# Four 64x64-tile matmuls a pick, and no VectorE adds, for the value rows of a two-layer decoder trunk

## The reference, cut to what matters

```python
def peer_ffn(h, w_q, sub_keys, u_tab, v_tab):
    ...   # scores against two sets of 128 keys, top 16 of each, top 16 of their sums:
    experts = i1 * PEER_KEYS + i2
    gates = jax.nn.softmax(best_s, axis=-1)
    ...   # chunks of 128 tokens, hk = 8 heads * 16 picks = 128
    def chunk(args):
        hh, ee, gg = args
        u_sel = u_tab[ee].astype(jnp.float32)
        v_sel = v_tab[ee].astype(jnp.float32)
        act = jax.nn.gelu(jnp.einsum('td,tkd->tk', hh, u_sel))
        return jnp.einsum('tk,tkd->td', gg * act, v_sel)

for l in range(DEPTH):
    x = mixer_sublayer(x, ...)
    x = x + peer_ffn(rms_norm(x, norm2_g[l]), peer_wq[l], peer_keys[l], peer_u[l], peer_v[l])
```

## Time and profile before

| | |
|---|---|
| median of 3 runs | 1670.06 us (1668.13 to 1670.81) |
| the profiled execution's own time | 1670.59 us |
| its span, first to last instruction | 1668.8 us |
| TensorE busy, share of the span | 78% |
| VectorE | 72% |
| ScalarE | 26% |
| GpSimd | 41% |
| HBM read | 621.15 MB, 373 GB/s over the span |
| mean granted TensorE clock | 0.901 of 2.4 GHz |

### The profile page before, as it was taken

The page is one execution under the profiler, slowest core; times in us unless marked ns, Lnnn a source line. Parts: engine busy times, 40 slices in busy tenths (PEclk is TensorE's granted clock), DMA queues, the critical chain, the costliest instruction groups (busy, mean ns, idle before and its releaser), DMA issues. The chain is left out here.

```text
span 1668.8 us, 15094 instructions
## 1 busy us (share of the span) xinstructions
PE 1308.3 (78%) x4636; PEld 732.2 (44%) x4636; DVE 1209.0 (72%) x2831; ACT 432.8 (26%) x1021; POOL 677.2 (41%) x791
## 2 busy tenths in 40 slices
PE   7794776977696697878878777889878788776786
PEld 6664432433354344544355434545345433332332
DVE  3834999865599978767589987867679975555555
ACT  3211331341233321224133332135123321111111
POOL 6002223686175253344333243434432235444441
PEclk9898998988798898988989888989989979999999
DMA  9006998969998899999999999999999989999998
GB/s 387 18 29 265 418 374 334 392 258 367 421 407 351 328 420 419 420 421 419 420 398 420 411 345 420 420 419 420 420 401 420 402 319 422 420 419 420 420 420 334
DMA packets 86050, 623.21 MB, mean 373 GB/s; under 512 B 9808, under 2 KB 9808, under 8 KB 10960
## 3 DMA queue, kind: packets, MB, share of 16 engines
q0 software_dynamic: 73728, 536.90, 78.9%
q1 hardware_dynamic: 12240, 85.33, 12.5%
HBM read 621.15 MB, written 1.05 MB: 373 GB/s over the span
## 5 line engine op out<-in xcount | busy, mean ns | idle before, releaser
L1348 PE MATMUL acc<-slot,diag 128*128 128x512 f32 x1780 | 870.1, 644 | 226.9 <-ACT diag L734 226.9
L458 POOL DMA_INDIRECT slot<-experts,idx x512 | 577.9, 1129 | 950.3 <-PE acc L1348 785.4
L1041 DVE CUSTOM_DVE_ANT_0 slot<-slot,h 128x1024 f32<-128x1024 f32 x512 | 611.8, 1226 | 273.1 <-DMA slot<-experts,idx 271.5
L1348 PEld LDWEIGHTS acc<-slot,diag 128*128 128x128 f32 x1780 | 358.1, 207 | 689.4 <-issue 419.8
L734 ACT ACTIVATE diag<-cst,ge 128x128 f32<-128x128 f32 x445 | 144.2, 391 | 187.0 <-DVE ge L760 185.8
L725 ACT ACTIVATE ge<-ge 128x4 f32<-128x4 f32 x129 | 26.5, 205 | 466.0 <-DVE ge L1041 465.1
L1318 PE MATMUL PB<-hT,ring 128*128 128x128 f32 x1024 | 126.2, 284 | 4.6 <-ACT hT L698 4.1
L1318 PEld LDWEIGHTS PB<-hT,ring 128*128 128x128 f32 x1024 | 122.8, 200 | 6.5 <-ACT hT L698 5.5
L719 ACT ACT_TABLE_LOAD x31 | 39.8, 1283 | 203.1 <-DVE rs L1000 203.1
L1059 DVE SCALAR_TENSOR_TENSOR xs<-slot,ge,xs 128x1024 f32<-128x1024 f32 x67 | 86.1, 1285 | 2.4
L725 ACT ACT_TABLE_LOAD x56 | 71.8, 1283 | 29.3 <-DVE ge L1041 28.4
(11 more groups left out here) (229 smaller groups left out, 1148.4 us busy)
## 6 DMA issues: line engine op xcount, KB each, us to landing
ring<-weights SPq DMA_DIRECT2D x32, 1152.0 KB, 9.5
ring<-weights SPq DMA_DIRECT2D x28, 1024.0 KB, 9.2
slot<-weights SPq DMA_DIRECT2D x12, 1024.0 KB, 22.2
slot<-experts,idx POOLq DMA_INDIRECT x512, 16.1
sml<-small SPq DMA_DIRECT2D x2, 1160.0 KB, 10.0
xs<-x SPq DMA_DIRECT2D x2, 512.0 KB, 8.1
out<-xs SPq DMA_DIRECT2D x4, 256.0 KB, 5.1
tabp<-tabs SPq DMA_DIRECT2D x2, 268.0 KB, 9.2
```

What stands on the lines that cost most here:

```text
L458: pool.indirect_dma_start(out=slot[:, E % SLOTS, :], out_offset=None, in_=experts, in_offset=bass.IndirectOffsetOnAxis(ap=idx[:, n % 2, e: ...
L1041: ins = dve.tensor_tensor_reduce(u, u, h2[:, n % 2, :], 1.0, 0.0, ALU.mult, ALU.add, d[:, i:i + 1])
L1348: ins = pe.matmul(acc[:, half, :], diag[:, d % DIAGS, :], slot[:, E % SLOTS, D + half * 512:D + half * 512 + 512], start=(E % PICKS == 0), ...
```

## The change

- `added` returns only the last two picks of all: 65 picks go from VectorE to TensorE, each with a diagonal on ScalarE.
- The diagonal is folded: a new constant `fold` has two 64 x 64 identities one above the other, and a pick's matrix is 128 x 64. Its rows 0 to 63 are the diagonal for tokens 0 to 63, its rows 64 to 127 that for tokens 64 to 127.
- A pick is added by four matmuls of 64 x 64 stationary and 512 columns: token half i (rows of the array) and column half (columns of the array). Token half i goes to PSUM bank i, column half to partitions 0 to 63 or 64 to 127 of it. The last of the four tells `expert_done`.
- The drain puts this back: four adds of 64 partitions x 512 in place of two of 128 x 512.

```diff
-    routing, experts = False, {PICKS * STEPS - 2, PICKS * STEPS - 1}
-    for kind, a, b in ORDER:
-        if kind == "open":
-            routing = a == STEPS - 1
-        elif kind == "close" and not routing:
-            experts.add(experts_of(a, b)[-1])
-        elif kind == "mix" and a.startswith("route"):
-            routing = True
-    return experts
+    return {PICKS * STEPS - 2, PICKS * STEPS - 1}
...
-        diag = sb("diag", [P, DIAGS, P])
+        diag = sb("diag", [P, DIAGS, HALF])
...
-                    act.activation(diag[:, d % DIAGS, :], ident, ACT.Copy,
+                    act.activation(diag[:, d % DIAGS, :], c_("fold"), ACT.Copy,
...
                 for half in range(2):
-                    x_half = xs[:, n % 2, half * 512:half * 512 + 512]
-                    told(tt(x_half, x_half, acc[:, half, :], ALU.add), "drained")
+                    for i in range(2):
+                        x_part = xs[HALF * i:HALF * i + HALF, n % 2, half * 512:half * 512 + 512]
+                        ins = tt(x_part, x_part, acc[HALF * half:HALF * half + HALF, i, :], ALU.add)
+                    told(ins, "drained")
...
-                    for half in range(2):
-                        ins = pe.matmul(acc[:, half, :], diag[:, d % DIAGS, :],
-                                        slot[:, E % SLOTS, D + half * 512:D + half * 512 + 512],
-                                        start=(E % PICKS == 0), stop=(d + 1 == by_tensor(PICKS * (n + 1))),
-                                        skip_group_check=True)
+                    for i in range(2):
+                        rows = slice(HALF * i, HALF * i + HALF)
+                        for half in range(2):
+
+                            ins = pe.matmul(acc[HALF * half:HALF * half + HALF, i, :], diag[rows, d % DIAGS, :],
+                                            slot[rows, E % SLOTS, D + half * 512:D + half * 512 + 512],
+                                            start=(E % PICKS == 0), stop=(d + 1 == by_tensor(PICKS * (n + 1))),
+                                            skip_group_check=True)
                     ins.then_inc(S["expert_done"], 1)
...
+    put("fold", np.concatenate([np.eye(HALF)] * 2))
```

More of the change, by code:

```diff
@@ L25 @@
 KD = D // P
+HALF = P // 2
 SEQ = 256
@@ L53 @@
 for _name, _w in (("ident", P), ("mask", P), ("ones", P), ("band", 4 * P), ("prev", 64), ("first", 64),
-                  ("iota", TOPK), ("minus", HEADS), ("eps", 1)):
+                  ("iota", TOPK), ("minus", HEADS), ("eps", 1), ("fold", HALF)):
     CONST[_name] = (_at, _at + _w)
```

## The result

Median of five runs 1658.2 us (1656.39 to 1660.04) against 1668.13 us (1665.75 to 1670.81) of the kernel before, five runs of each: ratio 0.994, 95% interval 0.9928 to 0.9952. It is faster, by 10 us where 18 were forecast; 1658.2 lies in the range, 6 us above the predicted 1652.

What follows compares the result with a forecast made beforehand. DMA engines were taken as full at 420 GB/s in most slices, so gains come only from slices below that. The terms -6.0 - 1.8 - 2.5 - 3.6 + 1.0 - 6.4 + 1.4 sum to -17.9: predicted 1652 us, range 1640 to 1665.

Steps and rivals of the forecast that it cites:

- Quads 7 to 12: Quads 7 to 11 of n = 0: VectorE works without a gap, so removing five adds of 1.20 gives -6.0 us.
- The price of a pick: TensorE's adds: four tiles side by side make a pick cost 0.86 us in place of 1.71.
- rival 3: TensorE's four tiles take turns, a pick costs 3.43 us and TensorE bounds: some 2,200 us; chance 0.07.
- what would show it: Signs if right: TensorE's adds 430 to 450 us busy, 0.86 us a pick, drain waits near 0, among others.
- Rival 1: A pick still costs 1.71 us, from a halved clock or tiles two at a time: 1661 us; chance 0.17.
- The gathers behind: GpSimd's last gather ahead of the tables: quad 12's four picks done after 3.4 us, not three after 5.1: -1.8 us.
- GpSimd's tables: Layer 1's tables: five VectorE adds each hold GpSimd up by 0.8 to 1.0 us; -2.5 us, bounds -4.5 and 0.
- Quad 23 and the projection: Quad 23's add delays routing dots, three times: -3.6 us; query projection in n = 1 and n = 2 may lose clock: +1.0.
- The add of quad 22 gives nothing: Removing quad 22's add gains nothing, since VectorE then waits for TensorE's query projection and ScalarE's copy.
- The step ends: Ends of three steps: first gather 1.7 us sooner each, -1.3 more at n = 1's end from the drain: -6.4 us.
- The end: Last drain: four adds take 2.8 us in place of two at 1.41, with nothing to cover it: +1.4 us.
- Rival 2: VectorE and GpSimd meet elsewhere: a 6.59 us stall comes once more, no gain on the tables: 1661 us; chance 0.13.

Runs made afterwards that it cites:

- (2): The kernel before, with TensorE doing the 65 picks by its old two matmuls and nothing packed: 1666.05 us, ratio 0.9981 to the kernel before.
- (7): The changed kernel with four more matmuls of zeros after each pick, to double its price: 1673.88 us, ratio 1.0028 to the kernel before.
- experiments 3: The changed kernel with VectorE adding the last pick of quads 13 to 18 of n = 0, ahead of the dots: 1666.15 us, ratio 0.998.
- 4: As experiments 3, but each of the six adds stands behind the four dots of the next quad: 1660.81 us, ratio 0.9936 to the kernel before.
- experiments 8: The changed kernel with TensorE adding the picks of quad 22 ahead of the query projection, not behind it: 1656.56 us, ratio 0.9922.
- 9: The changed kernel with the picks ahead of the query projection for n = 2 and n = 3 alone: 1656.97 us, ratio 0.9933.
- second profile: The same changed kernel measured and profiled once more, nothing changed: 1659.34 us, ratio 0.9939 to the kernel before.
- experiment 12: The changed kernel with picks ahead of the projection (n = 2, 3), the last step's picks as before, and zero matmuls without a wait: 1652.91 us.

## Why the prediction was right, and where not

- **Quads 7 to 12, and what bounds there:** right. -6.0 forecast, -6.0 in both profiles, and 6.1 us come back when these five adds do.
- **The price of a pick:** its mechanism was right (0.86 forecast without the tail, 0.86 measured so at the high clock, 0.915 with the tail; rival 3 is out), and what would show it was not: 607 us busy, not 430 to 450. The estimate took the high clock throughout; the low one stood in the working only as a rival. The rule of the Trainium skill that it named (TensorE: Matmul & The Clock Gate, "Why this matters for your kernels") speaks of just this: gaps send TensorE back to half rate. The trace agrees, with a mean clock of 0.83 in place of 0.901. Rival 1 took it as halved everywhere; it was so in part. Its time was too low, too: it gave 1661 us for the old price of a pick, and the two experiments with that price took 1666 (2) and 1674 (7).
- **The gathers behind:** -1.8 forecast, -1.4 and -0.9 measured; with the price doubled the term turns to +4.0, from -6.1 to -2.1, where the rival had +0.5.
- **GpSimd's tables:** mis-sized. -2.5 with a bound of -4.5 was forecast, -8.6 and -6.3 measured. The step that failed is "each holding GpSimd up by 0.8 to 1.0 us": besides its own hold, an add ahead of the dots makes them hold more, 15 to 17 operations in the stretch against 10 to 13 without adds (experiments 3 and 4). How it does so is open.
- **Quad 23 and the projection:** -3.6 and +1.0 forecast. Both parts show. The projection takes 6.63 us in n = 1 and 5.92 in n = 2, 5.57 and 5.18 before, and from w(., 22) to w(., 23) 1.1 and 0.8 us are lost; from w(., 23) to w(., 24) the 1.2 us of the add are gained (-16.0 to -17.2, and -15.6 to -16.9). In n = 0 quad 23 gains 1.4 us. But then quad 25 loses 4.9 and 4.2 us in the first profile, 3.3 and 3.7 in the second. The step that failed is that the gain of quad 23 was taken as kept in n = 1 and n = 2, where the mixing quads were called "as full" throughout: the DMA engines run short behind the projection, before as well, and a wait for rows at quad 25 was put at nothing. "The add of quad 22 gives nothing" held, as its slot stood fourth in line. This loss is the largest thing that the prediction didn't see; it comes with the packing and experiments 8 and 9 take it away, and what lies between the packing and the late rows is open.
- **The step ends:** -6.4 forecast; -1.7, -3.2 and -3.1 measured (-8.0; the second profile -2.1, -2.7, -2.7). The drain waits went to 2.54 us (n = 0) and 1.51 (n = 1), not near 0, for the low clock: where quad 31's picks ran at the high one (experiment 12) they are 0.04.
- **The end:** +1.4 forecast, +1.3 measured.
- **Rival 2** did not come: VectorE's one stall of 6.59 us became two, of 2.83 and 4.78 us, in the same part of n = 0.

The measured terms of the first profile, -6.0 - 1.4 - 8.6 + 9.1 - 8.0 + 1.3 = -13.6, make nearly all of the -14.4 of the span. Two errors partly met: 4 to 6 us too little at the tables, and 7 to 9 us of loss at quad 25 not seen. That the total came within 4 us of the forecast -17.9 is luck to that extent. The median lies 1.8 us above the profiled execution, and the forecast had put it 0.5 below, which makes up the rest of the 6.

## What to carry to other kernels

When work moves from one engine to another, follow each gain to the next place where the transfers run short, since it can be lost there. When two traces are compared, line them up by the work and not by the clock: a window at the same time shows other work once one kernel is 17 us ahead. Cost a long operation on VectorE by what it does to GpSimd through the operations behind it as well, and measure that by putting it back in another place. And where TensorE's share falls, take durations at both clocks for what stands behind its idle times; what counted here was when a pick was done behind an idle time, and not how many could be done in the whole.

## What the runs showed that was not expected

- Tiles that are a part of the array both ways run four at a time in float32: a pick of four 64 x 64 x 512 matmuls took 0.86 us (0.915 with the tail), where one of two 128 x 128 x 512 took 1.71 (1.78).
- Packing TensorE's adds from 1.96 to 1.19 us a pick gave 39% of their busy time, not half: the mean clock fell from 0.901 to 0.83, and rose again to 0.923 when zeros brought the price back to 1.89. Even so that version was 14.5 us slower.
- The stretch of the tables differs by 2 us or more from run to run with the same code, by how small operations on GpSimd meet long ones on VectorE.
- The same six adds on VectorE cost 7 to 8 us ahead of the dots and nothing that the runs can tell behind them.
